# Six modulation blocks summed by GpSimd instead of VectorE, and hosted by other projections

## The reference

```python
proj = jnp.einsum('bsd,df->bsf', h, w_in)            # 1024 -> 5 * 1536
q, f_f, f_b, i, gate = _split(proj, (C_WIDTH,) * 5)
def forget(z):
    f = lb + (1.0 - lb) * jax.nn.sigmoid(z)
    return heads(1.0 - f), heads(jnp.log(f))
k_f, g_f = forget(f_f)
k_b, g_b = forget(f_b)
o = bidirectional_gated_scan(qh, k_f, g_f, k_b, g_b, heads(i))
y = _head_rmsnorm(o, norm_gain) * jax.nn.silu(gate)
```

```python
c_act = jax.nn.silu(c)
mod = c_act @ w_ada[l] + b_ada[l]                    # 1024 -> 6 * 1024
sh_m, sc_m, g_m, sh_f, sc_f, g_f = [m[:, None, :] for m in jnp.split(mod, 6, -1)]
```

## Time and profile before

| | |
|---|---|
| median of 3 runs | 2505.05 us (2503.65 to 2507.1) |
| the profiled execution | 2502.24 us, its span 2500.4 us |
| granted TensorE clock, mean | 0.98 of full speed |
| PE busy | 95% of the span |
| DVE busy | 30% |
| ACT busy | 17% |
| POOL busy | 2% |

### The profile page before, as it was taken

How to read it: one execution, slowest core, us unless ns; L and a number is a source line. 1 busy time by engine, 2 the same in 40 slices (tenths; PEclk the granted TensorE clock), 3 DMA queues, 4 the chain that set the end, 5 groups by cost and what they waited for, 6 DMA issues and landing times.

```text
span 2500.4 us, 35576 instructions
## 1 busy us (share of the span) xinstructions
PE 2369.1 (95%) x15435; PEld 1395.5 (56%) x15435; DVE 743.0 (30%) x1657; ACT 431.1 (17%) x905; POOL 48.2 (2%) x67
## 2 busy tenths in 40 slices
PE   7999899999999899999999999899999999999998
PEld 5755667756676447777776744544434334443433
DVE  2372576453444514233035543300001000000001
ACT  1322123323312411000033232200000000000000
POOL 3400000000000000000000000000000000000000
PEclk9999999999999999999999999899999999999999
DMA  8953553332322128757223211399999999999997
GB/s 265 209 195 143 201 215 138 133 117 101 92 80 102 68 101 301 267 209 266 89 98 86 102 70 66 140 409 409 401 399 392 405 405 409 408 401 409 409 399 274
DMA packets 210444, 586.52 MB, mean 235 GB/s; under 512 B 14672, under 2 KB 16800, under 8 KB 210288
## 3 DMA queue, kind: packets, MB, share of 16 engines
q1 hardware_dynamic: 206512, 576.93, 61.9%
q0 software_dynamic: 3376, 5.94, 1.3%
q10 hardware_dynamic: 400, 1.36, 0.2%
HBM read 583.14 MB, written 1.06 MB: 234 GB/s over the span
## 4 chain that ended last, share of the span: by engine, by line
PE 78%; DMA 8%; DVE 7%; ACT 3%; SPq 2%; DVEq 1%; issue 1%; ACTq 0%
PE PSB L2768 14%; PE PSA L375 10%; PE PSA L393 8%; PE PSB L2672 8%; DMA RING<-in_w_moe 6%; PE PSB L2777 5%; PE PSA L2802 4%; PE PSA L2650 4%; PE PSA L752 4%; PE PSA L2033 2%; PE PSA L1903 2%; SPq L3082 2%; PE PSA L2816 2%; PE PSB L2629 1%; PE PSB L1537 1%
## 5 line engine op out<-in xcount | busy, mean ns | idle before, releaser
L2768 PE MATMUL PSB<-RING,Y 128*64 128x512 f32 x1792 | 401.0, 600 | 29.7 <-DMA RING<-in_w_moe 18.1
L375 PE MATMUL PSA<-RING,HT 128*128 128x512 f32 (+1 forms) x704 | 307.2, 589 | 13.3 <-ACT small L351 7.7
L2768 PEld LDWEIGHTS PSB<-RING,Y 128*64 128x64 f32 x1792 | 134.8, 138 | 267.8 <-issue 264.9
L393 PE MATMUL PSA<-HT,RING 128*128 128x256 f32 x1216 | 277.2, 388 | 6.9 <-DMA RING<-in_w_in_ab 4.5
L393 PEld LDWEIGHTS PSA<-HT,RING 128*128 128x128 f32 x1216 | 233.9, 195 | 41.9 <-issue 10.0
L375 PEld LDWEIGHTS PSA<-RING,HT 128*128 128x128 f32 x704 | 132.3, 193 | 156.0 <-issue 142.6
L2802 PE MATMUL PSA<-RING,ROW 128*64 128x512 f32 x896 | 198.6, 595 | 6.4 <-issue 5.1
L2672 PE MATMUL PSB<-HT,RING 128*128 128x256 f32 x896 | 199.0, 380 | 1.6 <-issue 1.6
L2672 PEld LDWEIGHTS PSB<-HT,RING 128*128 128x128 f32 x896 | 169.2, 190 | 30.7 <-issue 9.0
L2924 DVE TENSOR_TENSOR PROJ<-PROJ,PSB 128x512 f32<-128x512 f32 x28 | 18.2, 684 | 553.9 <-PE PSB L2768 553.9
L2777 PEld LDWEIGHTS PSB<-RING,Y 128*32 128x32 f32 (+1 forms) x3136 | 107.5, 114 | 51.7 <-issue 41.5
(11 more groups left out here) (470 smaller groups left out, 2246.7 us busy)
## 6 DMA issues: line engine op xcount, KB each, us to landing
RING<-in_w_moe SPq DMA_DIRECT2D x166, 2048.0 KB, 19.7
RING<-in_w_ada SPq DMA_DIRECT2D x24, 2048.0 KB, 8.8
RING<-in_w_dense SPq DMA_DIRECT2D x21, 2048.0 KB, 8.3
RING<-in_w_in SPq DMA_DIRECT2D x20, 2048.0 KB, 8.0
RING<-in_w_in_c SPq DMA_DIRECT2D x15, 2048.0 KB, 7.9
RING<-in_w_in_ab SPq DMA_DIRECT2D x10, 2048.0 KB, 18.8
RING<-in_w_out SPq DMA_DIRECT2D x4, 2048.0 KB, 8.0
RING<-in_w_out_ab SPq DMA_DIRECT2D x3, 2048.0 KB, 8.1
```

Of the source, the lines that this page charges most:

```text
L375: mm = pe.matmul(PSA[:, lane[k], 512 * t:512 * t + cols], HT[:, c, P * t:P * t + P], W[:, c, 0:cols], start=(c == 0), stop=(c == KC - 1))
L393: mm = pe.matmul(PSA[:, lane[k], S * j:S * j + S], W[:, c, P * j:P * j + P], HT[:, c, :], start=(c == 0), stop=(c == KC - 1))
L2768: mm = pe.matmul(WIDE_BANKS[i][WIDE * which:WIDE * which + WIDE, :], HTG[:, c, WIDE * which:WIDE * which + WIDE], W[which][:, c - per * kh ...
```

## The change

Blocks 6 to 11 are summed by POOL in a new function, `pool_sum_ada`. It scales all eight chunks in place, one operation each, and adds them as a tree of three operations over 4, 2 and 1 chunks. It posts to a semaphore of its own, for which `ada_columns` waits. The hosts of the six blocks are now (0, 0), (0, 2), (0, 4), (1, 1), (1, 3) and (2, 0). ACT's copies move with them. The six `sum_ada` calls on DVE go. POOL's rows of gains are issued partly between its sums.

```diff
+        POOL_SUMS = range(6, 12)
...
-        C_GROUP = [[hosting(0, 6 + i, w_c, 1536 * j) for i, j in enumerate((1, 2, 0, 3, 4))]]
-        C_GROUP += [[hosting(0, 11, w_c, 1536 * j + 512 * g) if (g, j) == (1, 4) else columns(w_c, 1536 * j + 512 * g, 512)
-                     for j in (1, 2, 0, 3, 4)] for g in range(1, 3)]
+        GUESTS = {(0, 0): 6, (0, 2): 7, (0, 4): 8, (1, 1): 9, (1, 3): 10, (2, 0): 11}
+        C_GROUP = [[hosting(0, GUESTS[g, i], w_c, 1536 * j + 512 * g) if (g, i) in GUESTS else columns(w_c, 1536 * j + 512 * g, 512)
+                    for i, j in enumerate((1, 2, 0, 3, 4))] for g in range(3)]
...
         def ada_columns(pe, l, j, to):
...
-            pe.wait_ge(sem("ada_summed"), ADA_ORDER.index((l, j)) + 1)
+            k = ADA_ORDER.index((l, j))
+            if k in POOL_SUMS:
+                pe.wait_ge(sem("ada_summed_pool"), POOL_SUMS.index(k) + 1)
+            else:
+                pe.wait_ge(sem("ada_summed"), k + 1 - len([i for i in POOL_SUMS if i < k]))
...
+        def pool_sum_ada(pool, l, j):
+
+            n = ADA[l][j]
+            wait_item(pool, n)
+            W = view(n)
+            for c in range(KC):
+                pool.tensor_scalar(W[:, c, :], W[:, c, :], cT[:, c:c + 1], None, ALU.mult)
+            for k in (4, 2, 1):
+                pool.drain()
+                e = pool.tensor_tensor(W[:, 0:k, :], W[:, 0:k, :], W[:, k:2 * k, :], ALU.add)
+            e.then_inc(sem("ada_summed_pool"), 1)
...
-            sum_ada(dve, 0, 6)
...
-            sum_ada(dve, 0, 7)
...
-                else:
-                    sum_ada(dve, 0, 8)
                 forget(g, 1)
-                for j in ((9, 10), (11,), ())[g]:
-                    sum_ada(dve, 0, j)
...
-            for n in range(len(row_list)):
+            for n in range(3):
+                pool_row(pool, n)
+            pool.wait_ge(sem("c_ready"), 1)
+            for k in POOL_SUMS:
+                if k == 8:
+                    for n in range(3, 5):
+                        pool_row(pool, n)
+                elif k == 11:
+                    pool_row(pool, 5)
+                pool_sum_ada(pool, *ADA_ORDER[k])
+            for n in range(6, len(row_list)):
                 pool_row(pool, n)
```

More of the change, by code:

```diff
@@ L1129, in act_second @@
                 take(act, C_GROUP[g][0], c_g[0], func=ACT.Exp, scale=-1.0, cols=S, tokens=False)
-                if g == 0:
-                    act_ada(act, C_GROUP[0][1])
+                if g == 1:
+                    act_ada(act, C_GROUP[1][1])
                 if g:
@@ L1145, in act_second @@
                 take(act, C_GROUP[g][2], c_q, func=ACT.Silu, cols=S, tokens=False)
-                if g == 0:
-                    act_ada(act, C_GROUP[0][3])
+                if g == 1:
+                    act_ada(act, C_GROUP[1][3])
                 act_gla_exp(act, 1 + g, 1.0)
                 take(act, C_GROUP[g][3], c_v)
-                if g < 2:
-                    act_ada(act, C_GROUP[g][4])
+                if g == 0:
+                    act_ada(act, C_GROUP[0][4])
                 if g:
@@ L1154, in act_second @@
                 take(act, C_GROUP[g][4], c_gate, func=ACT.Silu)
+                if g == 1:
+                    act_ada(act, C_GROUP[2][0])
             for g in range(2):
```

## The result

| | before | after |
|---|---|---|
| median of 20 runs | 2503.62 us | 2511.76 us |
| lowest to highest | 2500.88 to 2507.1 | 2505.07 to 2515.46 |
| ratio, 95% interval | | 1.0029 (1.0023 to 1.0035) |
| profiled execution | 2502.24 us | 2506.98 us |

The change made the kernel slower; I had forecast 2500 us, slightly faster. The profiled execution of the kernel after is the third fastest of its 20, so a second one was traced later (2511.62 us).

A forecast was written before the change was run, and what follows sets the result against it. PE was taken to be bound by three waits due to DVE, 16 us with clock. Gains of 4.2 and 0.5 us off 2502.24 gave 2497.5, plus 2.8 to the median: 2500 us, range 2494 to 2507 (8 in 10: 2486 to 2518).

The forecast's parts named there:

- The three waits: PE idle before (0, 2) and in the middle of (0, 4) and (1, 4): 9.96 us, plus 6.0 us of clock.
- The price of a sum on POOL: At MEMSET's rate, eight two-pass scalings of 7.3 us and three-pass additions of 8.8 us: 16.1 us per sum.
- The gap: Block 8 lands at 315.3 us, its host (0, 4) starts at 334.6 us: 19.3 us for the sum; sum 11 the same.
- at 16.1 us POOL is in time everywhere: Sums 8 and 11 have about 19 us, sums 7, 9 and 10 25 us or more, so PE never waits for POOL.
- my first sign of being wrong: The prediction called itself wrong if PE waits for POOL at L341, where the guest columns need the sum.
- The pace of DVE beside a sum: DVE assumed at half pace while POOL sums, halfway between losing nothing and standing still; reciprocal at full pace.
- My 19.5 us: Time from the preparation's start to ACT's take of v in the kernel before (330.80 to 350.33 us), used for both groups.
- the second rival: DVE and POOL hold each other, DVE falls below half pace in the preparation: slower, 2513 to 2537 us; chance 0.26.
- Group 0: PE waits 4.8 us in the middle of (0, 4); the group ends at 355.9 us instead of 360.1: 4.2 us gained.
- Group 1: (2, 0) starts at +88.8 us instead of +91.8, 3.0 us gained, of which 0.5 us stays after clock and guest.
- below half pace: Rival: DVE and POOL hold each other in the preparation; at a third of pace 2523 us; chance 0.26.
- the sum too long for its gap: Rival: a 24 us sum makes PE wait 4.7 us before (0, 4) and (2, 0), giving 2502 us; chance 0.08.

The follow-up runs named there:

- e1_no_pool_work: The kernel after with POOL computing none of the six sums, only posting them, so the modulation is wrong; second-layer stretch 247.3 us against 263.7 us before.
- e5_short_adds: The kernel after with each sum's three additions cut into seven of 512 elements, computing everything; ratio to before 1.0007 (0.9998 to 1.0016), stretch 264.9 us.
- e3_add_only: The kernel after with only the three additions of each sum on POOL, scalings left out, modulation wrong; ratio to before 0.9997, stretch 263.7 us.
- e2_scale_only: The kernel after with only the eight scalings of each sum on POOL, additions left out, modulation wrong; stretch 247.2 us against 263.7 us before.

## Why the prediction was wrong

**What bounds the kernel: right.** The three waits with their clock are 16 us; the kernel without POOL's work and the one with the sums in DVE's idle time both win 16.4 to 16.6 us in the stretch.

**The price of a sum on POOL: this is the step that failed.** I put a pass per operand at the rate of MEMSET: 7.3 us for the eight scalings, 8.8 us for the additions, 16.1 us. The additions were right (8.7 us). The scalings were not: 12.4 us, 1.57 us each instead of 0.91. This is the row of all 48 of them:

```profile
L375 POOL TENSOR_SCALAR RING<-RING,small x48: 1554/1568/2501, 224.5 to 437.9; 128x512 f32<-128x512 f32 x48
```

A sum alone is 21.2 us. Beside DVE's preparation it is 23.4 to 24.3 us: I let only DVE be slowed, and POOL is slowed too. The gap was sized about right (19.3 us forecast, 20 us measured). So "at 16.1 us POOL is in time everywhere" turned into 3.25 us of wait before (0, 4), and POOL stood beside DVE's chain half as long again as I had it. A wait of PE for POOL at L341 was my first sign of being wrong, and it came.

**The pace of DVE beside a sum: near in size, as a mean.** I took one half. In group 0 the preparation takes 29.9 us to v's take (318.11 to 348.04 us) instead of 19.5, with 24.8 us of sums beside it: 10.4 us lost, a pace of 0.58. In group 1 it is 30.5 us (420.38 to 450.86 us), with 24.3 us of sum 11: 11.0 us lost, 0.55. The preparation's starts and v's takes in the kernel after:

```profile
318.11 1.27 DVE L587 TENSOR_TENSOR_SCAN RING<-CF,PROJ 128x256 f32<-128x256 f32 x2 [1.12 <-ACT PROJ L1157]
...
420.38 1.27 DVE L587 TENSOR_TENSOR_SCAN RING<-CF,PROJ 128x256 f32<-128x256 f32 x2 [1.12 <-ACT PROJ L1157]
```

```profile
348.04 1.00 ACT L423 ACTIVATE PROJ<-PSA 128x1024 f32<-128x1024 f32 x1
...
450.86 1.00 ACT L423 ACTIVATE PROJ<-PSA 128x1024 f32<-128x1024 f32 x1
```

Some of this loss is not POOL's. In `e1_no_pool_work`, where POOL does nothing, the two preparations take 21.8 us (319.70 to 341.54 us) and 21.5 us, because without sums ahead of it DVE waits for ACT's exponentials (2.19 us in group 0). My 19.5 us was the length behind two sums, and about 2 us short of what the change would leave. Against that run POOL costs 8.1 and 9.0 us, a pace of 0.67 and 0.63.

The kind was wrong, too: not an even half, but nearly nothing beside scalings (with them alone the preparations take 22.0 and 22.8 us), and all of an addition. The Trainium skill's rule, page "SBUF — State Buffer", section "Who interferes with whom", which I had set beside the second rival, is half borne out. For additions the trace agrees: one operation of L589 takes 4.94 us. It also agrees that the reciprocal, with one input, isn't held (6552 to 6554 ns). That a GpSimd operation holds for its whole length is not borne out for scalings: an operation of L630 loses at most 0.43 of a scaling's 1.57 us.

**Group 0: right in its end, by luck.** Forecast 355.9 us, measured 356.1 us. But the wait in the middle is 0.47 instead of 4.8 us, because PE has already waited 3.25 us for POOL and run more slowly behind that (9.86 instead of 7.11 us), neither of which I had.

**Group 1: wrong by 7 us.** Forecast was the start of (2, 0) at +88.8 us, measured is +95.8 us (451.96 - 356.13). Block 10 landed at +36.2 instead of +31.9 us, because (1, 0) was held up 2.06 us by a mask behind sum 9's additions, which I had not counted, and ran on at a lower clock (0.91 from 368.0 to 386.6 us). Sum 10 so ended later, and one of its additions held L1199, the first operation of the second `forget`, for 2.6 us. The preparation started at +64.3 instead of +60.2 us. From there v's take began after 30.5 us, where I had 27.6 us: it stood beside 24.3 us of sum 11, not 16.1.

With a sum of 24 us and a pace of 0.55 to 0.58 on my 19.5 us, my own working for the two groups comes to an estimate of 2505 to 2507 us, about no change. So the term that failed explains 5 to 7 of the 12 us between the forecast and the median. I put the rest down to the mask and L1199, which my working did not have; no run takes them out by themselves. Of the second trace's 9.4 us over before, 7.0 lie in the stretch, 0.6 ahead of it and 1.8 behind it, and the last two I can't explain.

**The rivals.** What happened is between two: the slower one ("below half pace") in its sign and place, and the sum too long for its gap, in its cause. I had given the latter 0.08 and worked it out without the former. Either can be enough by itself: additions alone, never late, take back all of the gain, and so do sums of 27 and 28 us that hardly hold DVE. In the kernel after neither is alone. Its sums of 23.4 and 24.3 us miss the gap of 20.2 us by 3.2 and 4.1 us; at the 2.7 us of clock behind each wait of `e5_short_adds` (17.6 us over `e1_no_pool_work`, 12.2 of them waits) that is an estimate of 13 of the 20 us for lateness alone. The two losses don't add, because DVE's lateness and POOL's overlap in the same waits.

## What to carry to other kernels

Before work is moved to another engine, look for the places where its own engine waits on the same path: here DVE had 5 to 7 us of idle time between masks, and three sums there and one ahead of the first `forget` won 16 us, where moving them to POOL lost 8. A block in a ring has a gap from its landing to its use; an engine that misses it by 3 us costs that and the clock behind it. If POOL must work beside a busy DVE, give it operations with one input, or try those with two in short pieces: 512 elements instead of 2048 at most won 5 us here, though in group 0 it won nothing and in group 1 the additions happened to fall behind the chain. And measure the engine's own operation before pricing it: a write of MEMSET said 0.91 us for a scaling that took 1.57 us.

## What the runs showed of the hardware

- POOL scales 128x512 f32 in place in 1.57 us, more than three times DVE's 0.48 us; it adds 2048, 1024 and 512 elements per partition in 4.5, 2.35 and 1.26 to 1.53 us. At 2048 elements that is 2.2 ns per element, so scaling, with 3.1 ns, costs more per element than adding.
- POOL's additions hold those DVE operations that were seen with two SBUF inputs, and also its scalar operation and copies within SBUF (L1199 in the kernel after, L1203 and L593 in `e3_add_only`), for up to the whole addition (4.7 us on one L633); the reciprocal was never held (6552 to 6554 ns).
- Beside scalings of 1.57 us, DVE's operations in `e2_scale_only` took up to 0.43 us (L630) and 0.46 us (L623) longer; L607 and L608, which also read two tiles in SBUF, kept their 676 to 693 ns.
- Holding goes both ways: eight scalings took 12.4 us alone and up to 16.8 us beside DVE (`e5_short_adds`).
- With the additions in seven pieces instead of three, POOL's adding time alone grew from 8.7 to 9.2 us, each piece held one operation of DVE for 1.0 to 1.1 us in group 0, and the take of v in group 1 came 11.8 us earlier, 3.9 us of it before its preparation began.
